# Where the scan's decay matrix gets its running sums: broadcast on TensorE, or loaded broadcast from DRAM

## The reference, cut to what matters

```python
acs = jnp.cumsum((dt * a_neg).reshape(b, nc, q, g, e), axis=2)      # running sums in a chunk of 128 tokens
diff = acs[:, :, :, None] - acs[:, :, None, :]
lmat = jnp.exp(jnp.where(tril, diff, -jnp.inf))                     # decay matrix, 128 x 128 for each head
cb = jnp.einsum('bclgn,bcsgn->bclsg', cm, bm)
y_diag = jnp.einsum('bclsg,bclsge,bcsgep->bclgep', cb, lmat, xdt)   # inside the chunk
st = jnp.einsum('bclgn,bclge,bclgep->bcgepn', bm, decay_out, xdt)   # what the chunk adds to the state
y_off = jnp.einsum('bclgn,bcgepn,bclge->bclgep', cm, prev, jnp.exp(acs))
```

## Time and profile before

| | us |
|---|---|
| median of 3 runs | 2184.31 |
| lowest and highest of them | 2182.64, 2186.98 |
| span of the profiled execution, first to last instruction | 2188.3 |
| the profiled execution's own device time | not listed; the span is 3.99 above the median |
| TensorE matmul busy (2043.4) | 93% of the span |
| VectorE, ScalarE, GpSimd busy | 48%, 37%, 11% |
| chain that ended last: TensorE, VectorE, ScalarE | 75%, 10%, 7% |
| the scan's eight prompt chunks, first transpose of chunk 0 to first transpose of the sample chunk | 1520.2 to 1824.0 |

### The profile page before, as it was taken

How to read it: one execution, slowest core, us unless ns; L and a number is a source line. 1 busy time by engine, 2 the same in 40 slices (tenths; PEclk the granted TensorE clock), 3 DMA queues, 4 the chain that set the end, 5 groups by cost and what they waited for, 6 DMA issues and landing times.

```text
span 2188.3 us, 35605 instructions
## 1 busy us (share of the span) xinstructions
PE 2043.4 (93%) x14571; PEld 1944.9 (89%) x14571; DVE 1056.1 (48%) x2058; ACT 805.3 (37%) x1730; POOL 238.7 (11%) x358
## 2 busy tenths in 40 slices
PE   5999999999999999999999789999999978979997
PEld 4899999999889999999999689768999978979997
DVE  5214676525553535353356852564443466454523
ACT  5223444223533333324643111554445463122202
POOL 1001121100001010112222000001111111100000
PEclk9999999999999999999999887999999989989998
DMA  6211233201111111112275763574232435554422
GB/s 209 87 60 60 61 101 95 84 28 51 37 53 49 53 49 63 59 65 88 71 230 190 215 192 117 179 250 143 96 128 78 168 135 173 186 164 153 137 86 103
DMA packets 166995, 248.77 MB, mean 114 GB/s; under 512 B 19702, under 2 KB 114614, under 8 KB 166806
## 3 DMA queue, kind: packets, MB, share of 16 engines
q1 hardware_dynamic: 144576, 179.51, 26.3%
q0 software_dynamic: 22256, 66.98, 8.6%
HBM read 179.74 MB, written 66.70 MB: 113 GB/s over the span
## 4 chain that ended last, share of the span: by engine, by line
PE 75%; DVE 10%; ACT 7%; issue 4%; DMA 4%; SPq 0%; POOL 0%; DVEq 0%; ACTq 0%; POOLq 0%
PE bank L2277 18%; PE bank L2278 18%; PE bank L2279 18%; PE bank L2473 2%; DMA acc<-acc_T 2%; DVE w_lo L1710 2%; PE bank L2448 2%; PE bank L2431 1%; PE bank L2697 1%; PE bank L2409 1%; ACT soft L1511 1%; DVE softT L1969 1%; PE bank L2512 1%; ACT Lm L1637 1%; PE bank L2538 1%
## 5 line engine op out<-in xcount | busy, mean ns | idle before, releaser
L2277 PE MATMUL bank<-w_hi,hT_hi 128*128 128x256 f32 (+1 forms) x1848 | 533.3, 289 | 1.6 <-DVE hT_lo L2147 1.6
L2278 PE MATMUL bank<-w_lo,hT_hi 128*128 128x256 f32 (+1 forms) x1848 | 521.5, 282 | 0.0
L2279 PE MATMUL bank<-w_hi,hT_lo 128*128 128x256 f32 (+1 forms) x1848 | 520.8, 282 | 0.0
L2277 PE MATMUL bank<-hT_hi,w_hi 128*128 128x352 f32 x1344 | 458.1, 341 | 6.1 <-DVE acc L2124 5.7
L2278 PE MATMUL bank<-hT_lo,w_hi 128*128 128x352 f32 x1344 | 445.3, 331 | 0.0
L2279 PE MATMUL bank<-hT_hi,w_lo 128*128 128x352 f32 x1344 | 445.0, 331 | 0.0
L2277 PEld LDWEIGHTS bank<-w_hi,hT_hi 128*128 128x128 f32 (+1 forms) x1848 | 346.2, 187 | 3.3 <-issue 1.8
L2279 PEld LDWEIGHTS bank<-w_hi,hT_lo 128*128 128x128 f32 (+1 forms) x1848 | 347.4, 188 | 0.7
L2278 PEld LDWEIGHTS bank<-w_lo,hT_hi 128*128 128x128 f32 (+1 forms) x1848 | 346.2, 187 | 0.8
L2277 PEld LDWEIGHTS bank<-hT_hi,w_hi 128*128 128x128 f32 x1344 | 264.2, 197 | 9.3 <-DVE acc L2124 6.3
L2278 PEld LDWEIGHTS bank<-hT_lo,w_hi 128*128 128x128 f32 x1344 | 264.6, 197 | 1.4
(11 more groups left out here) (437 smaller groups left out, 3159.8 us busy)
## 6 DMA issues: line engine op xcount, KB each, us to landing
w_raw<-in_w_in SPq DMA_DIRECT2D x96, 512.0 KB, 4.7
kvring<-in_cache_win_kv SPq DMA_DIRECT2D x144, 256.0 KB, 3.5
feat_T<-fstage POOLq DMA_DIRECT2D x40, 528.0 KB, 3.4
fstage<-feat_T SPq DMA_DIRECT2D x16, 528.0 KB, 4.4
kvring<-in_cache_mem_kv SPq DMA_DIRECT2D x32, 256.0 KB, 3.5
xc<-feat_T SPq DMA_DIRECT2D x8, 1024.0 KB, 5.3
o_rows<-obuf POOLq DMA_DIRECT2D x48, 132.0 KB, 2.0
mo<-o_rows SPq DMA_DIRECT2D x24, 264.0 KB, 3.9
```

The source lines that it names most:

```text
L2277: pe.matmul(out, xh(k), wh(k), start=(k == 0), stop=False)
L2278: pe.matmul(out, xh(k), wl(k), start=False, stop=False)
L2279: ins = pe.matmul(out, xl(k), wh(k), start=False, stop=(k == nk - 1))
```

## The change

`ssd_dA` gets one more product, `dA` as the stationary operand and `upper` as the moving one, which gives the running sums turned: 128 rows (8 chunks by 16 heads) by 128 tokens, in bank 7. VectorE copies them to `yraw[:, 0:P]`. SyncE, at chunk 0, waits for that, stores them to a DRAM tensor `sum_T`, waits for the store and for the tail's stores that read `Lm`, and then loads the chunk's 16 rows into `Lm` broadcast over the 128 partitions (1 MB written). For chunk `c` it does the load right behind the load of `xc`. The prompt chunks' sixteen broadcast products are gone; ScalarE waits for the load, and its Relu reads `Lm` and writes it in place. The sample chunk stays as it was. TensorE's wait for the last Relu, ahead of the transposes of step 6, becomes a wait for the copies of `xtok`, which free banks 3 and 4.

```diff
+        sumT = dram("sum_T", [NB * SH, P])
...
+        s_sums = sem("s_sums")
@@ block.sync, step 3 of the chunk before (chunk 0: step 0)
                     if c < NB:
                         sp.dma_start(xc[:, :, :], featT[0:16, :, P * c:P * c + P].rearrange("f p n -> p f n")).then_inc(s_xc, 16)
+                        if c == 0:
+                            sp.wait_ge(s_s0, 4)
+                            sp.dma_start(sumT, yraw[:, 0:P]).then_inc(s_sums, 16)
+                            sp.wait_ge(s_sums, 16)
+                            sp.wait_ge(s_tls, 16 * 9)
+                        else:
+                            sp.wait_ge(s_dy, c)
+                        sp.dma_start(Lflat, sumT[SH * c:SH * c + SH, :].rearrange("h l -> (h l)").partition_broadcast(P)).then_inc(s_sums, 16)
@@ block.scalar, steps 1 and 2
                         for qq in (2 * q - 2, 2 * q - 1):
-                            act.wait_ge(s_dD, 4 * c + qq + 1)
-                            if qq == 0 and c == 0:
-                                act.wait_ge(s_tls, 16 * 9)
-                            elif qq == 0:
-                                act.wait_ge(s_dy, c)
-                                if c == NB:
+                            if c < NB:
+                                act.wait_ge(s_sums, 16 * (c + 2))
+                            else:
+                                act.wait_ge(s_dD, qq + 1)
+                                if qq == 0:
+                                    act.wait_ge(s_dy, c)
                                     act.wait_ge(s_fst8, 16)
                             l = Lm_of(c, qq)
+                            later = l if c < NB else D_of(c, qq)
                             for h in range(4):
-                                ins = act.activation(l[:, h, :], D_of(c, qq)[:, h, :], ACT.Relu, scale=-1.0,
+                                ins = act.activation(l[:, h, :], later[:, h, :], ACT.Relu, scale=-1.0,
@@ block.vector, ssd_dA
                     dve.wait_ge(s_ft, 1)
+                    dve.tensor_copy(yraw[:, 0:P], bank[7][:, P:2 * P])
@@ block.tensor, ssd_dA
+                    pe.matmul(bank[7][:, P:2 * P], dA[:, 0:P], table("upper"), start=True, stop=True)
@@ block.tensor, steps 1 and 2
-                    elif q in (1, 2):
-                        up = (table("upper") if c < NB else table("upper_s"))[0:m, 0:m]
+                    elif q in (1, 2) and c == NB:
+                        up = table("upper_s")[0:m, 0:m]
@@ block.tensor, step 6
                         if c < NB - 1:
-                            pe.wait_ge(s_ddf, 4 * c + 8)
+                            pe.wait_ge(s_dxt, c + 2)
```

## The result

The changed kernel takes 2206.09 us (median of 4 runs, 2201.39 to 2207.93), the kernel before 2185.64 (4 runs, 2182.64 to 2190.0). The ratio is 1.0083, with a 95% interval from 1.0061 to 1.0106: slower by about 18 us (the two medians lie 20.5 apart).

The account below looks back on a forecast made before the run. It took TensorE to bound each chunk's second part, and TensorE and a ScalarE-VectorE chain, nearly level, the first. Terms summed to 6.3 us gained less 10.0 for the clock: 2184.3 + 3.7 = 2188.0 us, range 2174 to 2197.

Parts of the forecast that it names:

- What bounds the first part: From a chunk's first transpose to its products with Lm: TensorE and the ScalarE-VectorE path nearly level, 0.67 us apart in chunk 2.
- the chain: ScalarE and VectorE work from a chunk's first transpose to VectorE's last product with CBm: 18.70 us before in chunk 2.
- Relu from SBUF: ScalarE's sixteen Relus a chunk read SBUF instead of PSUM: 0.7 us a chunk dearer, bounds nothing and twice 0.4.
- The load: 1 MB of sums a chunk behind xc: lands 8.5 us after issue, hidden except at chunk 7, which loses 2.0 us.
- Rival 4: The load of the sums comes late and ScalarE waits in each chunk: 14 us slower, 2202; chance 5%.
- Chunk 6: ScalarE already the bound there: Relu costs 0.8 us, the transposes leave the path, net 0.5 us lost.
- TensorE's clock: New stalls ahead of the products with Lm halve the clock: 2.0 us lost in each of five chunks, 2.1 in chunk 7.
- rival 2: The clock stays down for two stretches: six falls at 3.4 us each, slower by 12.0 us, 2196.3; chance 20%.
- the prediction's own sum: Gains and losses over the chunks: +6.3 us gained, less 10.0 for the clock in five chunks: slower by 3.7 us.

## Why the prediction was wrong

I said 2188.0, with 2174 to 2197 as the range; it is 2206.09. Step by step:

- *What bounds the first part* was right in chunks 0 to 5. The products with Lm start where the chain puts them: 20.5, 19.3, 19.3, 18.7 and 19.3 us after the first transpose in chunks 1 to 5, against 19.5 and 18.9 forecast. Chunk 4 gained 7.0 (6.8 forecast), chunk 0 3.7 (3.3). The stalls in chunks 2 to 5 are 3.0 to 3.7 us, where 3.3 to 4.2 were forecast; chunk 1's is 4.85.
- *Relu from SBUF* was right: 388 ns against 365 in the earlier trace rows, and a group of four takes 1.26 us in place of 1.12, some 0.6 a chunk where I took 0.7.
- *The load* is hidden but for two places. It lands 7.6 us after its issue (8.5 forecast), and the first part of chunk 7 pays 1.9 for its place in the queue (2.0 forecast), of which only 0.6 came back for the whole chunk when the order was changed. I missed the late weights of chunk 1, 0.9 us. Rival 4 did not occur.
- *Chunk 6* was wrong: "the transposes leave the path: -0.5". Its first part got 1.6 shorter and its second 4.9 longer. Before, VectorE's last product with CBm ended 20.0 us after the first transpose and TensorE started the products with Lm 2.2 later, held up by its transposes and state products at half clock; all of these 2.2 went, against 0.5 for the dearer chain. TensorE stood 10.36 us ahead of the products with Lm there, and I had priced no fall behind it.
- *TensorE's clock* is the step that failed: "I take 2.0, by the stall nearest in form", and 2.1 for chunk 7, 12.1 in all. The second parts grew by 5.0, 4.4, 3.4, 4.7 and 4.6 us in chunks 1 to 5 and by 4.9 and 4.7 in chunks 6 and 7: 31.6. The place and the sign were right. The size was wrong, and so was the upper bound of 3.4, and with it rival 2 ("each of the six falls costs 3.4"). I had read both ends from stalls with other work around them. The stall of 3.35 us, from which the 2.0 came, is not the start of a fall. The clock was at half from 1759.8 on, behind a wait of 2.40 us, and my 3.9 us were only the end of that stretch:

```profile
1759.00:1760.00 1.00, 0.00 (x0) 0.00 (x0) 0.31 (x1) 0.99 (x4) 0.00 (x0) 0.90 0.00 0
1760.00:1761.00 1.00, 0.26 (x1) 0.26 (x2) 0.39 (x1) 0.97 (x4) 0.00 (x0) 0.50 0.00 0
```

The whole stretch, 1759.8 to 1770.0, is as long as the one in chunk 2 of the changed kernel, 1614.3 to 1624.5, of which 9.0 us are work. And I took the 32 products behind the new stalls for dense work: "here it is dense". They fill TensorE's time, but with 64 columns each the clock stayed down through them, but for chunk 3. Widened to 128 columns in the same place, they bring the loss to 1.6 to 2.8, about what I had put in; that this then fits my 2.0 is luck, as the 2.0 was misread.

Put into the prediction's own sum, 31.6 in place of 12.1 makes 19.5 us more: 2184.3 + 3.7 + 19.5 = 2207.5, against 2206.09. That it comes out so near is partly luck: the first parts gained 10.9 us, where the sum had 8.4, the rest of the traced span was 4.0 shorter for no cause that I know, and the kernel before came out at 2185.64.

## What to carry to other kernels

Before taking work from an engine, read from one period who comes last and who comes second to last: the removed 3.8 us of a chunk could gain only the 0.7 between the two, whatever the engine's busy share. On TensorE, price the new stall as well: find in the trace where the granted clock falls and where it returns, not only where the stall ends, and look for work of the same width as that which will stand behind the new stall. When work has left a stage, fit the order of the steps to it and move other real, wide work into the hole; here that turned 18 us lost into 22 gained, and the same order without the removal gained nothing.

## What the runs showed of the hardware

- Thirty records of 16 columns and thirty of 128 take nearly the same time (3.45 and 3.51 us), and the profile counts TensorE busy in both. Towards the end of the narrow ones the clock fell to 1.2 GHz, through the wide ones it held 2.4 (chunk 2).
- In chunk 2, behind a stall of 3.65 us, 32 records with 64 columns take 7.09 us and end at half clock; behind one of 3.64, with 128 columns, they take 5.41 and end at full clock. At full clock throughout, those with 64 take 3.7. In chunk 3, behind stalls as long, they take 5.62 and 6.45.
- A fall does not need a long stall right ahead: behind a wait of 0.63 us the clock fell while records with 64 columns ran (chunk 7 with unread products of 128 columns).
- A stall of 2.99 us (chunk 4) cost as much as those of 3.6: 4.7 us. The Trainium skill, TensorE: Matmul & The Clock Gate, "Why this matters for your kernels", warns of gaps between bursts of matmuls. The trace agrees: the clock fell in or right behind each of the seven stalls of 2.99 to 10.36 us.
- Relu over 128x128 takes 388 ns from SBUF and starts every 0.29 us, 365 and 0.255 from PSUM. The Trainium skill, ScalarE: Activation LUTs, "What ACT_TABLE_LOAD costs", gives for an instruction with a bias operand 280 ns and 0.833 for each element of a row. By it 387 ns is the estimate for 128 elements, and the trace agrees for SBUF.
